# Modulation from the condition: plain fp32 products in four column tiles, the matrix in its own buffers

## The chip, the cores and the metric

One core of a Trainium2 chip runs the whole program. The metric is the device time of one execution in microseconds; lower is better. Three runs were made of the kernel before.

## The reference

Two transformer blocks on one sequence of 512 tokens of width 1024, all in fp32. The first block has two attentions (rotary differential and chunk-banded), a gated merge, cross attention to 256 memory tokens, a SwiGLU layer of width 2816 and a norm. The second block is modulated by a condition:

```python
mod = jax.nn.silu(c) @ w_ada[l] + b_ada[l]          # c: 1 x 1024, w_ada: 1024 x 6144
mod_c = jax.nn.silu(c_ctx) @ w_ada[l] + b_ada[l]    # the same matrix for the context
sh1, sc1, g1, sh2, sc2, g2 = jnp.split(mod[:, None, :], 6, axis=-1)
...
h_lat = _rms_norm(x, norm_mix[l]) * (1.0 + sc1) + sh1
```

It has a long convolution whose filter is made by a small sine network, a bidirectional gated linear attention, a projection, and a squared-ReLU layer of width 4096. What the change touches is `mod` and `mod_c`: two vectors of 1024 times one matrix of 1024 x 6144 (25.2 MB), whose result is needed first when the second block's first norm is applied.

## The kernel before, in words

Every large matrix goes through one path. It is cut into slabs of 128 columns with up to eight 128-row tiles (512 KB); a `Unit` is one slab. `U_` holds all units in the order in which every engine takes them. A slab goes through a ring of three slots:

- SP loads it into `raw` (`load`, line 509), once GpSimd is done with the slot's earlier slab (`low_done`).
- ScalarE rounds it to fp32r, `WH` (`high`, line 571), once TensorE is done with the slot (`unit_done`).
- GpSimd makes the rest, `WL = raw - WH` (line 552).
- TensorE adds up three products per row tile in fp32r: WH with the activation's high part, WH with its low part, WL with its high part (`unit`, line 1062): 24 products of 512 columns for a full slab. `half` (line 1074) and `piece` (line 1088) are the same in pieces.

The stages run one after the other. The stage `gu` (gate and up matrices of the SwiGLU layer) has 44 slabs, `dn0`, `dn1` and `dn2` (the down matrix) have eight each. After each `gu` unit VectorE takes the result from PSUM, scales it (lines 1942, 1944), ScalarE applies the silu (line 797), VectorE multiplies (line 1947), ScalarE and VectorE split the product into `fH` and `fL` (lines 800, 1648).

The modulation is done in the same ring. `w_ada` is the stage `ada` of 48 slabs, each two 128-row tiles of 512 columns. In `order` (lines 354 to 361) one `ada` unit stands behind each of the 44 `gu` units and behind the first four of `dn0`. The condition's silu, `cS` (128 x 8 x 2: vector and context), is split by VectorE into `cR`, high and low part, four columns (lines 1723 to 1725). TensorE's `ada(i)` (line 1366) multiplies each row tile of the slab's WH and WL by these four stationary columns, with 512 moving columns, into PSUM bank 5: four products a unit, and four units make one block of 512 columns. ScalarE's `keep_rows` copies the 4 x 512 result (line 788), sends it to DRAM (line 790), and reads all back at `dn0`'s fifth unit, turned so that 48 partitions have 128 columns each (line 825). After `dn1` TensorE transposes it (line 1411), and VectorE adds the bias and the low part's row (lines 1998, 2000).

At the border from the first block's cross attention to `gu`, TensorE waits for sums, then does the first `gu` unit in pieces (line 1088) and the statistics' sum (line 1035); ScalarE and VectorE finish the statistics, and ScalarE makes no weight copy until it has the square root (line 602). In `dn0` the filter network runs between the units: ScalarE issues the loads of its weights on its own DMA queue when `dn0`'s first unit is over (lines 806 to 812), and TensorE does its first product after the second unit (`filter_mm`, line 1374), the next ones after the fourth and sixth (line 1377), each behind a sine of ScalarE (line 821).

Other lines that the prediction names: 1187 (scores of the first attention, plain fp32: two products, one on partitions 0 to 63 and one on 64 to 127, into two banks), 1291 and 1310 (cross attention, plain fp32), 1525 (scores of the linear attention), 1543 (its states: plain fp32, 64 x 64 stationary, output on partitions 0 to 63 and 64 to 127 of bank 2 in turn, 128 columns), 1537 (128 x 128, before and behind 1543), 1420 (column sums, plain fp32, one moving column).

Of the kernel before, what the change touches and what calls it, by code (L numbers as in the profile page):

```python
# [22 lines left out]
ALU = mybir.AluOpType  # L23
# [42 lines left out]
SLOTS = 3  # L66
SLAB_KT = 8
# [49 lines left out]
def build(nc, t, out):  # L117
    ctx = ExitStack()
    with ctx:
# [32 lines left out]
        cR = place("cR", [P, DT, 4], F32R)  # L152
# [32 lines left out]
        rows = [z(f"rows{i}", kb, [4, S]) for i, kb in enumerate((93, 89))]  # L185
        mod_rows = hz("mod_rows", 0, [48, 4, P])
# [106 lines left out]
        mod_dram = nc.dram_tensor("mod_rows_dram", (4, 6 * D), F32, kind="Internal")  # L293
# [9 lines left out]
        def pairs(even, odd):  # L303
# [25 lines left out]
            Stage("ada", 48, DT, lambda i: w_ada[:, 2 * (i % 4):2 * (i % 4) + 2, i // 4 * S:(i // 4 + 1) * S]),  # L329
# [24 lines left out]
        for s_ in stages:  # L354
            if s_.name in ("gu", "dn0"):

                first = 0 if s_.name == "gu" else st["gu"].n
                for i in range(s_.n):
                    order.append((s_, i))
                    if first + i < st["ada"].n:  # L360
                        order.append((st["ada"], first + i))
            elif s_.name == "hyp":

                order += [(st[name], i) for name, i in WEAVE]
            elif s_.name == "ogp":
                order += [(s_, 0), (s_, 1), (st["grp"], 0), (s_, 2), (s_, 3)]
            elif s_.name not in ("ada", "uu", "grp"):
                order += [(s_, i) for i in range(s_.n)]
# [3 lines left out]
        for un in U_:  # L372
            if un.stage.name != "ada":
                un.out, un.bank = outs, un.stage.ring[made[un.stage.name] % len(un.stage.ring)]
                made[un.stage.name] += 1
                un.free = in_bank.get(un.bank, 0)
                outs += 1
                in_bank[un.bank] = outs
# [4 lines left out]
        def first_out(name):  # L383
# [22 lines left out]
        cond_ok, mod_in, mod_mm, lam_exp, lam_ok = (  # L406
            sem(n) for n in ("cond_ok", "mod_in", "mod_mm", "lam_exp", "lam_ok"))
        row_out = [sem(f"row_out{i}") for i in range(2)]
        scored, maxed, exped, normed, turned, kept, pv_done, pv_out = (
            {k: sem(f"{n}_{k}") for k in ("ab", "c")} for n in  # L410
            ("scored", "maxed", "exped", "normed", "turned", "kept", "pv_done", "pv_out"))
# [28 lines left out]
        def wide(a):  # L440

            return a[:].rearrange("p (a b) c -> p a (b c)", a=2)

# [14 lines left out]
        with_half = [g for g in range(STEPS) if g not in HEAD_STEPS]  # L458

# [25 lines left out]
        def _(sp):  # L485
# [15 lines left out]

            def load(lo, hi):
                for un in U_[lo:hi]:
# [4 lines left out]
                    dst = wide(raw[un.slot]) if s_.name == "ada" else raw[un.slot][:, 0:s_.kt, 0:width(s_)]  # L508
                    sp.dma_start(dst, s_.source(un.i)).then_inc(slab_in[un.slot], 16)
# [48 lines left out]
        def _(act):  # L558
# [221 lines left out]
            def keep_rows(i):  # L780

                if i % 4 == 3:
                    b = i // 4
                    if b >= 2:

                        act.wait_ge(row_out[b % 2], 16 * (b // 2))
                    act.wait_ge(unit_done, at["ada", i].u + 1)
                    act.activation(rows[b % 2][:], bank(5, S, 4), ACT.Copy).then_inc(row_kept, 1)
                    act.wait_ge(row_kept, b + 1)
                    act.dma_start(mod_dram[:, b * S:(b + 1) * S], rows[b % 2][:]).then_inc(row_out[b % 2], 16)  # L790

            for i in range(2 * FT):
# [8 lines left out]
                high(at["ada", i].u + SLOTS)  # L801
                keep_rows(i)
            for i in range(8):
# [11 lines left out]
                if i < 4:  # L815
                    high(at["ada", 2 * FT + i].u + SLOTS)
                    keep_rows(2 * FT + i)
# [201 lines left out]
        def _(pe):  # L1019
# [283 lines left out]
            def weigh_c(h):  # L1303
                pe.wait_ge(kept["c"], ST * (h + 1))
                if h:
                    pe.wait_ge(pv_out["c"], 2 * h)
# [11 lines left out]
            for s_ in range(C_ITEMS + 4):  # L1318
# [5 lines left out]
                if s_ == 10:  # L1324
                    begin(co0)
                    pe.wait_ge(pv_out["c"], 2)
# [4 lines left out]
                if s_ in (14, 16):  # L1331
                    pe.wait_ge(pv_out["c"], 4)
# [6 lines left out]
                if s_ == 18:  # L1339
                    for un in (co0, co1):  # L1340
                        pe.wait_ge(pv_out["c"], 6)
                        piece(un, oH, oL, (4, 5), 4, DT)

            pe.wait_ge(pv_out["c"], 2 * X_HEADS)
# [11 lines left out]
            def ada(i):  # L1356

                un = at["ada", i]
                pe.wait_ge(low_done, un.u + 1)
                if i % 4 == 0 and i:  # L1360

                    pe.wait_ge(row_kept, i // 4)
# [26 lines left out]
            pe.wait_ge(cond_ok, 1)  # L1389
            for i in range(2 * FT):  # L1390
# [5 lines left out]
                ada(i)  # L1396
            pe.wait_ge(res["gu"], 15)
            for i in range(8):
                unit(at["dn0", i], fH[:, 0:8], fL[:, 0:8])
                if i < 4:  # L1400
                    ada(2 * FT + i)
# [7 lines left out]
            pe.wait_ge(mod_in, 16)  # L1409
            for c in range(4):  # L1410
# [983 lines left out]
```

## Time and profile before

| | |
|---|---|
| median of 3 runs | 1798.88 us (1798.59 to 1800.63) |
| the profiled execution | 1800.05 us, span 1798.2 us |
| TensorE busy, products | 1729.0 us (96%) x7986 |
| VectorE | 895.9 us (50%) |
| ScalarE | 663.2 us (37%) |
| GpSimd | 770.9 us (43%) |
| mean granted TensorE clock | 0.984 |
| DMA | 179.86 MB, mean 100 GB/s |

The profile is one execution. Products on TensorE are pipelined: each is listed with its whole duration (0.39 us for one of 512 columns), and the next starts 0.23 us after it, so durations of neighbours overlap, and the distance from start to start is what one costs. The chain of waits follows the program back from its end: each piece is the instruction group that the next one waited for, or stood behind on its engine.

### The profile page before, as it was taken

What the parts mean: (1) busy time and instruction counts of PE and PEld (TensorE: products, weight loads), DVE (VectorE), ACT (ScalarE), POOL (GpSimd) and SP (SyncE); (2) the same over time, 40 slices, a digit from 0 to 9 for tenths busy, and PEclk for the clock granted to TensorE, in tenths of its full rate; (3) what the DMA queues carried; (4) which work ended last, traced back from release to release, by engine and by line L of the source; (5) the groups of instructions that cost most, each with busy time, mean ns of one, the idle gap of its engine ahead of it and who ended that gap; (6) DMA issues with size and microseconds to landing.
All of it is one profiled execution on the core that took longest, in us unless ns stands there. A gap on an engine that the chain in (4) does not pass through costs nothing.

```text
span 1798.2 us, 20290 instructions
## 1 busy us (share of the span) xinstructions
PE 1729.0 (96%) x7986; PEld 1354.5 (75%) x7986; DVE 895.9 (50%) x1233; ACT 663.2 (37%) x1036; POOL 770.9 (43%) x338
## 2 busy tenths in 40 slices
PE   5999999999999889999999998999999899999997
PEld 4777666677986667777777787787777688888886
DVE  5626656477424543333324655364565677162624
ACT  6124434355433434444442343463232323222222
POOL 2333222245741347777775333322133344444441
PEclk9999999999999989999999999999999899999999
DMA  5232211033541235555554222412034223333331
GB/s 186 74 90 71 59 47 51 27 123 106 156 137 47 59 94 164 165 164 168 163 170 136 82 72 78 145 53 59 24 88 126 85 83 102 97 94 95 104 95 59
DMA packets 293555, 179.86 MB, mean 100 GB/s; under 512 B 7961, under 2 KB 277811, under 8 KB 293204
## 3 DMA queue, kind: packets, MB, share of 16 engines
q1 hardware_dynamic: 291132, 170.63, 32.5%
q10 hardware_dynamic: 1768, 5.81, 1.0%
q0 software_dynamic: 560, 2.12, 0.3%
q8 instruction: 64, 1.05, 0.2%
q14 instruction: 31, 0.25, 0.0%
HBM read 174.22 MB, written 4.32 MB: 99 GB/s over the span
## 4 chain that ended last, share of the span: by engine, by line
PE 93%; DVE 3%; ACT 2%; issue 1%; DMA 1%; ACTq 0%; POOL 0%; DVEq 0%; SPq 0%
PE ps L1062 60%; PE ps L1074 13%; PE ps L1088 6%; PE ps L1366 2%; PE ps L1228 2%; PE ps L1196 1%; PE ps L1310 1%; PE ps L1208 1%; PE ps L1291 1%; PE ps L1187 1%; PE ps L1543 1%; PE ps L1141 0%; PE ps L1509 0%; DMA tok<-in_x_dram 0%; PE ps L1385 0%
## 5 line engine op out<-in xcount | busy, mean ns | idle before, releaser
L552 POOL TENSOR_TENSOR WL<-raw,WH 128x1024 fp32r<-128x1024 f32 (+2 forms) x330 | 768.5, 2337 | 987.8 <-ACT WH L571 987.6
L571 ACT ACTIVATE WH<-raw 128x1024 fp32r<-128x1024 f32 (+2 forms) x330 | 331.4, 1007 | 812.6 <-PE ps L1062 665.0
L1062 PE MATMUL ps<-hH,WH 128*128 128x512 f32 x808 | 205.9, 397 | 0.2 <-DVE qG L2051 0.2
L1062 PE MATMUL ps<-hL,WH 128*128 128x512 f32 x808 | 199.7, 389 | 0.0
L1062 PE MATMUL ps<-hH,WL 128*128 128x512 f32 x808 | 199.6, 389 | 0.0
L1062 PEld LDWEIGHTS ps<-hH,WH 128*128 128x128 f32 x808 | 150.8, 188 | 42.1 <-issue 3.8
L1062 PEld LDWEIGHTS ps<-hL,WH 128*128 128x128 f32 x808 | 151.0, 187 | 32.4
L1062 PEld LDWEIGHTS ps<-hH,WL 128*128 128x128 f32 x808 | 151.0, 187 | 32.2
L1074 PE MATMUL ps<-hH,WH 128*128 128x512 f32 x328 | 138.0, 421 | 0.7 <-DVE vfTc L2053 0.7
L1074 PE MATMUL ps<-hL,WH 128*128 128x512 f32 x328 | 129.1, 394 | 0.0
L1074 PE MATMUL ps<-hH,WL 128*128 128x512 f32 x328 | 129.0, 393 | 0.0
L1861 DVE SCALAR_TENSOR_TENSOR x<-ps,mod,x 128x512 f32<-128x512 f32 x40 | 30.0, 750 | 125.6 <-PE ps L1062 116.8
L1074 PEld LDWEIGHTS ps<-hH,WH 128*128 128x128 f32 x328 | 61.8, 188 | 32.4 <-issue 19.5
L1648 DVE TENSOR_TENSOR mL<-tmp,mH 128x512 fp32r<-128x512 f32 x32 | 78.0, 2438 | 7.6 <-ACT mH L1005 7.5
L1870 DVE TENSOR_TENSOR acc<-acc,tmp 128x512 f32<-128x512 f32 x40 | 67.5, 1689 | 28.6 <-ACT tmp L611 28.6
L1944 DVE TENSOR_TENSOR tmp<-ps,r 128x512 f32<-128x512 f32 x22 | 15.2, 691 | 118.8 <-PE ps L1062 118.8
L1074 PEld LDWEIGHTS ps<-hH,WL 128*128 128x128 f32 x328 | 62.0, 189 | 14.1
L1074 PEld LDWEIGHTS ps<-hL,WH 128*128 128x128 f32 x328 | 62.1, 189 | 10.9
L1062 PE MATMUL ps<-mH,WH 128*128 128x512 f32 x224 | 56.0, 392 | 0.0
L1062 PE MATMUL ps<-mH,WL 128*128 128x512 f32 x224 | 55.3, 389 | 0.0
L1062 PE MATMUL ps<-mL,WH 128*128 128x512 f32 x224 | 55.3, 389 | 0.0
L1648 DVE TENSOR_TENSOR fL<-tmp,fH 128x512 fp32r<-128x512 f32 x22 | 46.0, 2089 | 16.1 <-ACT fH L800 16.1
(461 smaller groups left out, 2767.8 us busy)
## 6 DMA issues: line engine op xcount, KB each, us to landing
raw<-in_w_in_dram SPq DMA_DIRECT2D x64, 512.0 KB, 3.6
raw<-in_w_mlp_dram SPq DMA_DIRECT2D x64, 512.0 KB, 3.9
raw<-in_w_ada_dram SPq DMA_DIRECT2D x48, 512.0 KB, 3.6
raw<-in_w_gate_up_dram SPq DMA_DIRECT2D x44, 512.0 KB, 3.6
raw<-in_w_out_dram SPq DMA_DIRECT2D x16, 512.0 KB, 3.7
raw<-in_w_ckv_dram SPq DMA_DIRECT2D x16, 512.0 KB, 3.9
raw<-in_w_down_dram SPq DMA_DIRECT2D x16, 448.0 KB, 3.5
raw<-in_k_dft_dram SPq DMA_DIRECT2D x17, 256.0 KB, 2.7
```

Of the source, the lines that this page charges most:

```text
L552: pool.tensor_tensor(WL[un.slot][:, 0:s_.kt, 0:n], raw[un.slot][:, 0:s_.kt, 0:n], WH[un.slot][:, 0:s_.kt, 0:n].bitcast(F32), ALU.subtract) ...
L571: act.activation(WH[un.slot][:, 0:s_.kt, 0:n], raw[un.slot][:, 0:s_.kt, 0:n], ACT.Copy).then_inc(high_done, 1)
L1062: ins = pe.matmul(dst, w[un.slot][:, q, 0:m], a[:, q, :], start=(k == 0), stop=(k == 3 * kt - 1))
L1074: ins = pe.matmul(bank(un.bank), w[un.slot][:, q, :], a[:, q, :], start=(q == 0 and e == 0), stop=(q == DT - 1 and e == 2))
L1088: ins = pe.matmul(bank(un.bank), w[un.slot][:, q, :], a[:, q, :], start=(c == 0 and e == 0), stop=(c == kt - 1 and e == 2))
L1187: ins = pe.matmul(ps[:, 3 + 2 * (n % 2) + c, 0:nk], qA[rows, h, q], kA[rows, h, 0:nk], start=True, stop=True)
L1196: ins = pe.matmul(bank(3 + n % 3, nk), qB[rows, h // 2, q], kB[rows, h // 2, 0:nk], start=True, stop=True)
L1228: ins = pe.matmul(ps[rows, 2, b * P:S], v[:, b, c], src[:, b, b * P:S], start=(b == 0), stop=True, skip_group_check=True)
L1366: ins = pe.matmul(bank(5, S, 4), cR[:, k, :], wide(w[un.slot])[:, q, :], start=(k == 0 and w is WH), stop=(k == DT - 1 and w is WL))
L1648: return dve.tensor_tensor(dl, src, dh.bitcast(F32), ALU.subtract)
L1861: dve.scalar_tensor_tensor(xm, bank(un.bank), scale(un.i), xm, ALU.mult, ALU.add).then_inc(bank_free, 1)
L1870: ins = dve.tensor_tensor(acc[:], acc[:], tmp[un.i % 2][:], ALU.add)
```

## The change

The stage `ada` leaves the slab ring, and its products become plain fp32 with the stationary operand `cS` itself (two columns; `cR` and its two VectorE instructions go). The matrix is loaded in twelve blocks of 512 columns, 2 MB each, into two buffers of 16 KB per partition (`ada_w`), which lie where `fH` and `fL` are written only late in the stage. SP issues each block as four transfers of 512 KB, two behind the load of a `gu` slab and two behind the next, for the slabs 3 to 26; from the third block on it first waits until TensorE is done with the block two before, and it waits until the block before has landed.

TensorE does a block at once after every second `gu` unit, from the fourth (i = 3) to the twenty-sixth (i = 25): 16 products of 256 columns. Four consecutive ones write to partitions 0, 32, 64 and 96 of bank 5: the even and odd row tile (q), each with the left and right half of the block (e). So each of the four places adds up four row tiles. `keep_rows` copies 128 x 256 and sends all of it to DRAM. The read back takes four transfers of the rows wanted, 24 partitions each, and the transposes become plain products with the identity that also add the even and odd part: eight where there were four. VectorE adds the bias in two instructions instead of four.

```diff
+ADA_PARTS = 12
-        cR = place("cR", [P, DT, 4], F32R)
-        rows = [z(f"rows{i}", kb, [4, S]) for i, kb in enumerate((93, 89))]
-        mod_rows = hz("mod_rows", 0, [48, 4, P])
+        rows = [z(f"rows{i}", kb, [P, 256]) for i, kb in enumerate((93, 89))]
+        mod_rows = hz("mod_rows", 0, [24, 8, P])
+        ada_w = [z(f"ada_w{i}", kb, [P, DT, S]) for i, kb in enumerate((28, 72))]
...
-            if s_.name in ("gu", "dn0"):
-
-                first = 0 if s_.name == "gu" else st["gu"].n
-                for i in range(s_.n):
-                    order.append((s_, i))
-                    if first + i < st["ada"].n:
-                        order.append((st["ada"], first + i))
...
+        def ada_after(i):
+            return i % 2 == 1 and 0 <= (i - 3) // 2 < ADA_PARTS
...
+            def load_ada(b, part):
+
+                if part == 0:
+                    if b < 2:
+                        sp.wait_ge(unit_done, first_u("gu"))
+                    else:
+                        sp.wait_ge(ada_done, b - 1)
+                    if b:
+
+                        sp.wait_ge(ada_in, 64 * b)
+                for k in (4 * part, 4 * part + 2):
+                    sp.dma_start(ada_w[b % 2][:, k:k + 2, :], w_ada[:, k:k + 2, b * S:(b + 1) * S]).then_inc(ada_in, 16)
...
+                    if s_.name == "gu" and 0 <= un.i - SLOTS < 2 * ADA_PARTS:
+                        load_ada((un.i - SLOTS) // 2, (un.i - SLOTS) % 2)
...
+            def keep_rows(b):
+
+                if b >= 2:
+
+                    act.wait_ge(row_out[b % 2], 16 * (b // 2))
+                act.wait_ge(ada_done, b + 1)
+                act.activation(rows[b % 2][:], bank(5, 256), ACT.Copy).then_inc(row_kept, 1)
+                act.wait_ge(row_kept, b + 1)
+                act.dma_start(mod_dram[:, b * 256:(b + 1) * 256], rows[b % 2][:]).then_inc(row_out[b % 2], 16)
...
-                high(at["ada", i].u + SLOTS)
-                keep_rows(i)
+                if ada_after(i - 1):
+                    keep_rows((i - 4) // 2)
...
-                    act.dma_start(mod_rows[:], mod_dram[:, :].rearrange("c (m p) -> m c p", p=P)).then_inc(mod_in, 16)
+                    for q in range(2):
+                        for e in range(2):
+                            first = 32 * (2 * q + e)
+                            act.dma_start(mod_rows[:, 4 * e + 2 * q:4 * e + 2 * q + 2, :],
+                                          mod_dram[first:first + 2, :].rearrange("c (m p) -> m c p", p=P)).then_inc(mod_in, 16)
...
-                for q in range(2):
-                    for w in (WH, WL):
-                        k = 2 * (i % 4) + q
-                        ins = pe.matmul(bank(5, S, 4), cR[:, k, :], wide(w[un.slot])[:, q, :],
-                                        start=(k == 0 and w is WH), stop=(k == DT - 1 and w is WL))
-                ins.then_inc(unit_done, 1)
+            def ada(b):
+
+                pe.wait_ge(ada_in, 64 * (b + 1))
+                if b:
+
+                    pe.wait_ge(row_kept, b)
+                for k in range(0, DT, 2):
+                    for q in range(2):
+                        for e in range(2):
+                            j = 32 * (2 * q + e)
+                            ins = pe.matmul(ps[j:j + 2, 5, 0:256], cS[:, k + q, :], ada_w[b % 2][:, k + q, e * 256:(e + 1) * 256],
+                                            start=(k == 0), stop=(k == DT - 2), skip_group_check=True)
+                ins.then_inc(ada_done, 1)
...
-                ada(i)
+                if ada_after(i):
+                    ada((i - 3) // 2)
...
-            for c in range(4):
-                ins = pe.transpose(ps[:, 5, c * 48:(c + 1) * 48], mod_rows[:, c, :], ident[0:48, 0:48])
+            for c in range(2):
+                for e in range(2):
+                    for q in range(2):
+                        ins = pe.matmul(ps[:, 5, c * 48 + e * 24:c * 48 + e * 24 + 24], mod_rows[:, 4 * e + 2 * q + c, :], ident[0:24, 0:24],
+                                        start=(q == 0), stop=(q == 1), skip_group_check=True)
```

## Rows read from the trace of the kernel before

**Rows 1.** The page, busy time of each engine (share of the span).

```profile
PE 1729.0 (96%) x7986; PEld 1354.5 (75%) x7986; DVE 895.9 (50%) x1233; ACT 663.2 (37%) x1036; POOL 770.9 (43%) x338
```

**Rows 2.** Who waited for whom, 640 to 1060 us: total, times, longest (us).

```profile
ACT WH L571 <- PE ps L1062: 219.9, 61, 8.6
...
PE ps L1366 <- POOL WL L552: 2.0, 1, 2.0
```

**Rows 3.** Chain of waits, 600 to 1100 us: start, us, what.

```profile
659.31 1.69 PE ps L1366 x4
661.00 6.47 PE ps L1062 x24
...
668.40 5.45 PE ps L1062 x24
673.85 0.93 PE ps L1366 x4
...
940.16 4.36 DMA fout<-in_filt_wout_dram
...
945.64 7.27 PE ps L1062 x24
```

**Rows 4.** By stretch: length, PE, PEld, DVE, ACT, POOL busy, clock, DMA share, GB/s.

```profile
670.00:930.00 260.00, 260.00 (x1142) 197.28 (x1142) 84.73 (x82) 109.62 (x132) 204.42 (x82) 1.00 0.55 165
960.00:964.00 4.00, 4.00 (x15) 2.55 (x15) 2.71 (x4) 1.87 (x3) 3.47 (x2) 1.00 0.97 312
```

**Rows 5.** Groups of instructions, 640 to 1060 us: busy us, mean ns, idle before.

```profile
L552 POOL TENSOR_TENSOR WL<-raw,WH 128x1024 fp32r<-128x1024 f32 (+1 forms) x114 | 279.2, 2467 | 145.7 <-ACT WH L571 145.7
L571 ACT ACTIVATE WH<-raw 128x1024 fp32r<-128x1024 f32 (+1 forms) x113 | 117.2, 1040 | 227.4 <-PE ps L1062 219.9 <-issue 4.3 <-DMA raw<-in_w_gate_up_dram 2.6
...
L1366 PE MATMUL ps<-WL,cR 128*4 128x512 f32 x96 | 38.5, 401 | 0.0
...
L788 ACT ACTIVATE rows<-ps 4x512 f32<-4x512 f32 x12 | 6.9, 572 | 0.0
```

**Rows 6.** Chain of waits, 520 to 556 us: plain fp32 passes on the whole array.

```profile
525.28 0.86 PE ps L1291 x4
...
551.92 3.44 PE ps L1310 x8
```

**Rows 7.** TensorE in order of time: start, us, line, shapes, passes.

```profile
203.99 1.13 PE L1187 MATMUL ps<-kA,qA 64*128 64x512 f32 x4
205.05 0.50 PE L1074 MATMUL ps<-hH,WH 128*128 128x512 f32 x1
205.39 0.40 PE L1074 MATMUL ps<-hL,WH 128*128 128x512 f32 x1
...
1271.43 0.38 PE L1537 MATMUL ps<-vG,att 128*128 128x128 f32 x2
1271.74 0.66 PE L1543 MATMUL ps<-state,qin 64*64 64x128 f32 x8
1272.33 0.38 PE L1537 MATMUL ps<-vG,att 128*128 128x128 f32 x1
```

**Rows 8.** In order of time: the first filter product and the first sine.

```profile
944.57 1.07 PE L1374 MATMUL ps<-zT,fw 33*64 33x512 f32 x2 [1.84 <-DMA fout<-in_filt_wout_dram]
...
954.93 0.61 ACT L821 ACTIVATE fh<-ft 64x512 f32<-64x512 f32 x1
```

**Rows 9.** Chain of waits: the transposes of the rows, and eight one-column passes.

```profile
1031.08 0.37 PE ps L1411 x4
...
1041.22 0.79 PE ps L1420 x8
```

**Rows 10.** TensorE in order of time, and one stretch, in the linear attention.

```profile
1258.81 2.05 PE L1525 MATMUL ps<-qin,kin 64*128 64x128 f32 x16
...
1265.02 2.05 PE L1525 MATMUL ps<-qin,kin 64*128 64x128 f32 x16 [1.22 <-DVE att L2184]
...
1267.00:1270.50 3.50, 3.50 (x10) 2.73 (x10) 1.98 (x3) 0.00 (x0) 0.00 (x0) 0.52 0.00 0
```

More of the change, by code:

```diff
@@ L366, in build @@
                 order += [(s_, 0), (s_, 1), (st["grp"], 0), (s_, 2), (s_, 3)]
-            elif s_.name not in ("ada", "uu", "grp"):
+            elif s_.name not in ("uu", "grp"):
                 order += [(s_, i) for i in range(s_.n)]
@@ L372, in build @@
         for un in U_:
[L373 to L378, printed above, removed]
+            un.out, un.bank = outs, un.stage.ring[made[un.stage.name] % len(un.stage.ring)]
+            made[un.stage.name] += 1
+            un.free = in_bank.get(un.bank, 0)
+            outs += 1
+            in_bank[un.bank] = outs
         def first_u(name):
@@ L405, in build @@
             sem(n) for n in ("rot_done", "roped", "v_turned", "v_kept", "sig_done"))
-        cond_ok, mod_in, mod_mm, lam_exp, lam_ok = (
-            sem(n) for n in ("cond_ok", "mod_in", "mod_mm", "lam_exp", "lam_ok"))
+        ada_done, mod_in, mod_mm, lam_exp, lam_ok = (
+            sem(n) for n in ("ada_done", "mod_in", "mod_mm", "lam_exp", "lam_ok"))
+        ada_in = sem("ada_in")
         row_out = [sem(f"row_out{i}") for i in range(2)]
-        scored, maxed, exped, normed, turned, kept, pv_done, pv_out = (
+        scored, maxed, exped, normed, turned, kept, pv_done = (
             {k: sem(f"{n}_{k}") for k in ("ab", "c")} for n in
-            ("scored", "maxed", "exped", "normed", "turned", "kept", "pv_done", "pv_out"))
+            ("scored", "maxed", "exped", "normed", "turned", "kept", "pv_done"))
+        pv_out = sem("pv_out")
         out_a, out_b = sem("out_a"), sem("out_b")
@@ L507, in load @@
                     s_ = un.stage
-                    dst = wide(raw[un.slot]) if s_.name == "ada" else raw[un.slot][:, 0:s_.kt, 0:width(s_)]
-                    sp.dma_start(dst, s_.source(un.i)).then_inc(slab_in[un.slot], 16)
+                    sp.dma_start(raw[un.slot][:, 0:s_.kt, 0:width(s_)], s_.source(un.i)).then_inc(slab_in[un.slot], 16)
+                    if s_.name == "gu" and 0 <= un.i - SLOTS < 2 * ADA_PARTS:
+                        load_ada((un.i - SLOTS) // 2, (un.i - SLOTS) % 2)
             load(0, first_u("gate"))
@@ L778, in _ @@
             stat("ffn", r)
[L780 to L790, printed above, removed]
+            def keep_rows(b):
[5 more added lines that the diff above has]
+                act.dma_start(mod_dram[:, b * 256:(b + 1) * 256], rows[b % 2][:]).then_inc(row_out[b % 2], 16)
             for i in range(2 * FT):
@@ L1720, in values @@
                 dve.wait_ge(v_turned, c0 + st[name].n)
-            dve.wait_ge(silu_c, 2)
-            own.step(dve.tensor_scalar(cR[:, :, 0:2], cS[:], 1.0, None, ALU.mult))
-            dve.tensor_tensor(cR[:, :, 2:4], cS[:], cR[:, :, 0:2].bitcast(F32), ALU.subtract).then_inc(cond_ok, 1)
             values("va", 0)
@@ L1915, in out_c @@
                     c = 2 * h + j
-                    rest(bank(b_), oH[:, c, :], oL[:, c, :]).then_inc(pv_out["c"], 1)
-                dve.wait_ge(pv_out["c"], 2 * h + 2)
+                    rest(bank(b_), oH[:, c, :], oL[:, c, :]).then_inc(pv_out, 1)
+                dve.wait_ge(pv_out, 2 * h + 2)
             each("cq", query_tile, 0, 3)
@@ L1997, in _ @@
             for c in range(2):
-                own.step(dve.tensor_tensor(mod[:, :, c], ps[:, 5, c * 48:(c + 1) * 48],
-                                           vec[:, VEC_AT["b_ada_2"]:VEC_AT["b_ada_2"] + 48], ALU.add))
-                ins = dve.tensor_tensor(mod[:, :, c], ps[:, 5, (2 + c) * 48:(3 + c) * 48], mod[:, :, c], ALU.add)
-                if c == 0:
-                    own.step(ins)
+                ins = dve.tensor_tensor(mod[:, :, c].rearrange("p (b e m) -> p e b m", e=2, m=2),
+                                        ps[:, 5, c * 48:(c + 1) * 48].rearrange("p (e b m) -> p e b m", e=2, m=2),
+                                        vec[:, VEC_AT["b_ada_2"]:VEC_AT["b_ada_2"] + 48].rearrange("p (b e m) -> p e b m", e=2, m=2),
+                                        ALU.add)
             ins.then_inc(mod_ok, 1)
```

31 lines of the change are left out of this document (9 added, 22 removed).

## The prediction

> **What bounds the kernel now.** I read the page's busy table first: TensorE is busy 96% of the span, no other computing engine over 50% [rows 1]. Busy alone decides nothing, so next came who waits for whom in the stretch that the change touches, 640 to 1060 us: the longest wait is one for TensorE (ScalarE's weight copies waited 219.9 us for products to free their slot), and TensorE's modulation products waited 2.0 us in all, for GpSimd [rows 2]. Then the chain of waits: from 661 to 935 us it is nothing but TensorE, a unit of 24 products at 5.45 us and four modulation products at 0.93 us in turn, without an issue gap [rows 3]. So in the gate/up stage TensorE's own time is the stage's time, and each microsecond taken out of it there leaves the path. GpSimd works 204 us of the 260 there and the DMA engines 0.55 of the time, at 165 GB/s [rows 4].
>
> **Removed on TensorE.** 192 modulation products of 512 columns with four stationary columns (96 on the high halves, as the 96 on the low ones in [rows 5]). On the chain they are 48 groups of four at 0.93 us [rows 3]: 44.6 us. One of them stands behind the pause of 2.0 us: it starts at 659.3, when GpSimd has its low half, and takes 1.69 in place of 0.93, the unit after it 6.47 in place of 5.45 [rows 2, 3]; they ran at half clock for a while. In the new order the three slots filled before the statistics are three gate/up units, 16 us of work for TensorE from about 651 us, and the fourth one's low half is there at 659.3, where the group's is now. Pause and slow stretch go: 2.0 + 0.8 + 1.0 = 3.8 us.
>
> **Added on TensorE.** Twelve bursts, one after every second unit from the fourth on. A burst is 16 plain fp32 products of 256 columns, and a plain fp32 product is two passes: 4 passes of 256 columns stand as 0.86 us, 8 of 512 as 3.44 us [rows 6], so 0.215 us a pass of 256 and half that for 128. 32 passes one behind the other are 6.88 us. The four products of a group write partitions 0, 32, 64 and 96, so they lie in four column tiles. The trace has no four tiles, but it has two. Line 1543 alternates between two column halves, with the same rows: eight passes of 128 columns (0.11 us each alone) take 0.59 us from start to next start, not 0.86; line 1187, with two row halves, takes 1.06 us for four passes of 512 columns where one behind the other they were 1.72 [rows 7]. Without the edges (below) that is half of the serial time: both tiles ran at once. In line 1187 that holds though the program issues each product's two passes one after the other. I take four tiles at once, as that is the same mechanism and the nearest row is column tiling in one bank: 8 slots of 0.215, 1.72 us. Bounds: no overlap, 6.88; two tiles only, 3.44.
> The Trainium skill ("TensorE: Matmul & The Clock Gate", Part 3, What overlaps) gives 2.38 times for three column tiles and 3.07 times for four row tiles, not 4; by the latter a burst's passes would be an estimated 2.24 us, and the sum 6 us worse.
> The edges: going from 128 columns to a narrower tile costs 0.09 us (1271.43, two passes, to 1271.74), the first load and the drain 0.15 (0.59 less four slots of 0.11), the first product back on the whole array 0.11 (205.05 to 205.39 against 0.23) [rows 7]: 0.35. A burst is 2.07 us, twelve are 24.8 us. The burst wants a pass every 0.054 us; line 1543's eight in 0.44 us came as fast.
>
> **The down stage.** Two groups stood before the first filter product. That product waits for its weights, whose transfer is issued by ScalarE behind nine small ones after the stage's first unit; it is issued at about 940.2, lands 4.36 us later, and TensorE had stood 1.84 us [rows 3, 8]. Without the two groups TensorE only comes 1.86 us earlier and stands 3.7: gain 0 (the landing may come up to 1.5 us sooner with less traffic: low end only). After the pause the unit takes 7.27 instead of 5.45 at half clock, today as well; I keep that. Two more groups are behind it: 1.86 of the 44.6 counts, 1.86 does not. Next the second filter product: its sine is done at 955.5 [rows 8] and it is wanted 5.45 us after the unit that ends at 952.9 [rows 3], so nothing is late.
>
> **Turning the rows.** Four transposes (0.37 us) become eight plain products, 16 passes; eight passes of one column took 0.79 us [rows 9], so 1.6, and 0.1 more of edges: +1.3 us, on the path in the down stage.
>
> **Costed at nothing.** GpSimd loses 48 low halves, ScalarE 48 copies: neither is on the path, gate/up units come every 5.45 us or more and need 2.5 and 1.0 [rows 5]. The row copy (0.57 us now, [rows 5]) follows the silu, some 2.2 us after the unit behind a burst; the next burst wants the bank 5.45 us after it: 3 us of cover; without it each burst would pay the difference. VectorE loses two conversions early on and two of four small sums late; ScalarE's queue gets four row reads where it had one, in a stage where it has one copy a unit to make. The new 1 KB rows for all partitions write 1.5 MB more.
> **Loads.** SP issues the same 48 modulation transfers of 512 KB, but in half the stage: four with every two slabs, behind the slab. SP then waits until the burst two before is done, and the next slab stands behind that wait and 1 MB. The slab is issued up to 4 us late and then stands behind that 1 MB: 1.5 MB are 5 us at the 300 GB/s that 165 at a share of 0.55 come to when full, so it lands within 8; ScalarE wants it 10.9 us after, TensorE two units later still. Twelve blocks and 24 slabs are 37.7 MB in 24 x 5.45 + 24.8 = 156 us: 243 GB/s, a share of 0.81 by the ratio of [rows 4]. The engines have carried 312 GB/s at 0.97 [rows 4]. Cover is there, but it is half gone.
>
> **Sum.** -44.6 - 3.8 + 24.8 + 1.9 (the two groups given back) + 1.3 = -20.4 us. Against the profiled execution's 1800.05 that is 1779.6; its time lies 1.2 above the median of the runs, 1798.88, so 1778.5.
>
> **Rivals.**
> *Only two tiles at a time* (each product's second pass holds up the ones behind it, or the four streams from the same partitions are too many). For: the trace has never more than two. Against: there both were fully at work [rows 7]. Then 3.44 + 0.35 = 3.79 a burst, 45.5 in all: 1799.2, the same. The Trainium skill says on that page that products start and end in strict order of the program; by that rule each second pass blocks the next product and this rival is the forecast. Line 1187's four passes in two slots disagree: by strict order they were three slots. 10%.
> *No overlap (the other side).* Products with the same 128 rows share one stream of weights and columns, and every burst costs 6.88 + 0.35 = 7.2 us: 86.8 in all, 1840.5. It decides from 3.77 us a burst on, the break-even (2.07 + 20.4 / 12). Against it: line 1543 has the same rows for both tiles. 5%.
> *The clock falls.* A burst fills 8 of 128 columns. Sixteen narrow passes (2.05 us) behind a pause of 1.22 us were followed by 3.5 us at 0.52 of the clock; the same sixteen without a pause kept the full clock [rows 10]. One such fall costs 1.75 us. If every second burst causes one, 10.5 us: 1789; if all, 1799.5. A burst has no pause beside it, which speaks against. 10%.
> *The loads become the bound.* If this mix of transfers gets only three quarters of the 300 GB/s, 225, the 37.7 MB take 168 us, 12 more: 1790.5. The 312 GB/s speak against. 4%.
>
> **Chances.** Forecast 71% (its own range 1771 to 1787: the landing 1.5 sooner, a burst cheaper by 0.2 or dearer by 0.5, one half-clock stretch of 1.75 more or two fewer at the pauses that stay); the rivals 10, 5, 10 and 4%. The range reaches 1771 to 1798, which takes in the loads and most of the clock. About 0.2%, 3.6 us, is what a measurement of this kernel tells from no change. Faster by over that: 0.71 + 0.04 + most of the clock = 0.85; same 0.09; slower 0.06.
>
> **What would show it.** The chain after: units of 5.45 us back to back and twelve bursts of about 2.07 (32 passes, starts in groups of four); 3.8 or 7.2 shows a rival. PEclk 1.0 through the stage, or not. DMA share near 0.8 over the first 24 units, 0.4 behind; gate/up slabs landing some 8 us after issue behind modulation loads, and no wait of TensorE for ScalarE's copies. The pause at 657 gone; the one before the first filter product longer by up to 1.9. I am wrong if TensorE shows waits inside the gate/up stage, or if a burst is much off 2 us.

## The result

The changed kernel takes 1779.9 us (median of five runs, the lowest 1778.71) against 1798.88 us for the one before; the ratio is 0.9888, with a 95% interval of 0.9875 to 0.9902. Forecast were 1778.5 us and a range of 1771 to 1798. One of the five, the one that was profiled, took 6667.16 us, with TensorE's products 0.84 us apart in place of 0.23 at a recorded clock of 1.00, for a reason that is not known. So all rows of the kernel after are from another execution of the same kernel (experiment 1 below): 1779.05 us, span 1777.2. The span before was 1798.2, so 21.0 us have to be accounted for.

The busy table and the slices of the page after; [rows 1] answer to them.

```profile
PE 1707.7 (96%) x8190; PEld 1346.0 (76%) x8190; DVE 891.9 (50%) x1229; ACT 614.4 (35%) x988; POOL 647.5 (36%) x290
...
PEclk9999999999999999999999999999999899999999
DMA  5232121134552157873333223421133233333331
```

TensorE is still busy 96% of a shorter span, so the kernel is bound as before; GpSimd and ScalarE lost their 48 conversions each; but for TensorE's old pause of 2.0 us for GpSimd, the time didn't come from there. The DMA row shows the loads crowded into the slices from 666 to 800 us and thinner behind. Next the chain of waits after, over the stretch that the change touches; [rows 3, 9] answer to it. It starts with the first gate/up unit, which is done in pieces (L1094).

```profile
642.44 6.45 PE ps L1094 x24
...
649.75 16.37 PE ps L1068 x72
666.11 1.84 PE ps L1372 x32
667.95 11.12 PE ps L1068 x48
...
808.67 1.84 PE ps L1372 x32
810.51 103.62 PE ps L1068 x456
...
918.99 4.25 DMA fout<-in_filt_wout_dram
923.28 1.07 PE ps L1380 x2
924.35 12.71 PE ps L1068 x48
937.06 1.00 PE ps L1383 x2
...
1007.91 1.89 PE ps L1418 x16
1009.80 9.74 PE ps L1068 x42
1019.55 0.79 PE ps L1428 x8
```

Behind it three units (72 products) run without a pause where the old one of 2.0 us was. Then comes a period that repeats: a burst of 32 passes (L1372), 1.84 us, and two units, 11.12 us, 12.96 in all. Two units cost 10.90 by [rows 3], so a burst costs 2.06 us. The twelfth starts at 808.67; from there TensorE has nothing but units. The two places of waiting that matter, TensorE's first filter product in order of time, then the whole waits over 640 to 1060 us ([rows 8] and [rows 2] answer to them):

```profile
923.28 1.07 PE L1380 MATMUL ps<-zT,fw 33*64 33x512 f32 x2 [3.73 <-DMA fout<-in_filt_wout_dram]
```

```profile
ACT WH L578 <- PE ps L1068: 269.3, 66, 11.0
POOL WL L559 <- ACT WH L578: 256.9, 69, 16.2
```

ScalarE waits for TensorE longer than before (269.3 us against 219.9) and GpSimd waits for ScalarE: both have more slack. The pause ahead of the filter product is 3.73 us, where it was 1.84. The stretches after, as in [rows 4]:

```profile
650.00:810.00 160.00, 160.00 (x979) 120.04 (x982) 56.31 (x53) 46.75 (x64) 60.99 (x26) 1.00 0.70 229
810.00:910.00 100.00, 100.00 (x451) 82.45 (x441) 37.66 (x37) 29.73 (x37) 43.90 (x19) 1.00 0.33 97
```

The clock is 1.00 through the bursts, TensorE is busy in every microsecond of it, and the DMA engines are at 0.70, not full.

### The profile page after: what moved, and what is told of

Its sections match the earlier page's. It is cut to its first block, busy times and chain, and to the rows that moved or that the text cites. A ratio compares the mean times of both kernels' runs of the same rounds, so it can differ in the third digit from the quotient of the medians.

```text
span 6665.3 us, 20564 instructions
## 1 busy us (share of the span) xinstructions
PE 6627.1 (99%) x8190; PEld 3652.8 (55%) x8190; DVE 848.3 (13%) x1229; ACT 622.2 (9%) x988; POOL 634.1 (10%) x290
## 4 chain that ended last, share of the span: by engine, by line
PE 99%; DVE 0%; ACT 0%; DMA 0%; issue 0%; ACTq 0%; SPq 0%; DVEq 0%
PE ps L1068 62%; PE ps L1080 16%; PE ps L1094 6%; PE ps L1234 2%; PE ps L1202 2%; PE ps L1214 1%; PE ps L1372 1%; PE ps L1193 1%; PE ps L1316 1%; PE ps L1297 1%; PE ps L1160 1%; PE ps L1147 1%; PE ps L1031 1%; PE ps L1168 0%; PE ps L1533 0%; PE ps L1391 0%
## 5 line engine op out<-in xcount | busy, mean ns | idle before, releaser
L1068 PE MATMUL ps<-hH,WH 128*128 128x512 f32 x808 | 770.8, 1205 | 0.0
L1068 PE MATMUL ps<-hH,WL 128*128 128x512 f32 x808 | 749.5, 1178 | 0.0
L1068 PE MATMUL ps<-hL,WH 128*128 128x512 f32 x808 | 749.2, 1176 | 0.0
L1068 PEld LDWEIGHTS ps<-hH,WH 128*128 128x128 f32 x808 | 392.8, 490 | 345.5 <-issue 340.3
L1068 PEld LDWEIGHTS ps<-hH,WL 128*128 128x128 f32 x808 | 398.8, 494 | 319.8 <-issue 319.8
L1068 PEld LDWEIGHTS ps<-hL,WH 128*128 128x128 f32 x808 | 398.0, 493 | 321.0 <-issue 321.0
L1080 PE MATMUL ps<-hH,WH 128*128 128x512 f32 x328 | 481.6, 1468 | 0.0
L1080 PE MATMUL ps<-hL,WH 128*128 128x512 f32 x328 | 456.5, 1392 | 0.0
L1080 PE MATMUL ps<-hH,WL 128*128 128x512 f32 x328 | 455.7, 1389 | 0.0
L1080 PEld LDWEIGHTS ps<-hH,WH 128*128 128x128 f32 x328 | 204.3, 623 | 231.9 <-issue 227.4
L1080 PEld LDWEIGHTS ps<-hL,WH 128*128 128x128 f32 x328 | 235.2, 717 | 103.7 <-issue 103.5
L1080 PEld LDWEIGHTS ps<-hH,WL 128*128 128x128 f32 x328 | 215.3, 656 | 127.9 <-issue 126.6
L1068 PE MATMUL ps<-mH,WH 128*128 128x512 f32 x224 | 193.4, 1104 | 0.0
L1068 PE MATMUL ps<-fL,WH 128*128 128x512 f32 x176 | 151.5, 1091 | 0.0
L1068 PE MATMUL ps<-fH,WH 128*128 128x512 f32 x176 | 151.4, 1092 | 0.0
L1068 PE MATMUL ps<-fH,WL 128*128 128x512 f32 x176 | 150.6, 1098 | 0.0
```

Of the source, the lines that this page charges most:

```text
L1068: ins = pe.matmul(dst, w[un.slot][:, q, 0:m], a[:, q, :], start=(k == 0), stop=(k == 3 * kt - 1))
L1080: ins = pe.matmul(bank(un.bank), w[un.slot][:, q, :], a[:, q, :], start=(q == 0 and e == 0), stop=(q == DT - 1 and e == 2))
```

## Where the 21.0 us went

By the two chains, from the start of one piece to that of the next (of the chain before, the pieces at 643.39, 960.22 and, [rows 9], 1041.22 us; after, at 642.44, 937.06 and 1019.55):

| from, to | before | after | difference | forecast |
|---|---|---|---|---|
| start to the first gate/up unit | 643.39 | 642.44 | -0.95 | 0 |
| from there to the second filter product | 316.83 | 294.62 | -22.21 | -21.7 |
| from there to the eight one-column passes behind the turned rows | 81.00 | 82.49 | +1.49 | +1.3 |
| the rest of the kernel | 756.98 | 757.65 | +0.67 | 0 |

The second row is all of the modulation, the pause at its start and the pause at the filter. The half microsecond by which it beats the forecast is at two stretches of half clock: in the first unit, 6.45 us where it was 6.71, and behind the filter's pause, 1.6 us lost where it was 1.8. The first and the last row, -0.95 and +0.67, hold next to nothing of the change (two conversions of VectorE early, two small sums late). They are of the size by which single executions differ: in the eleven traces here the piece of the first row starts between 642.44 and 645.11 us. Experiment 4 shows one place in the last row.

## The experiments

Each is timed beside runs of the kernel before on its own chip (medians 1799.5, 1799.3 and 1800.6 us in the three groups), so ratios are to be compared. Four questions: do all four tiles run at once, and on what does it depend (1 to 3, 9, 10); what does the filter's pause cost (4, 5); what do the small added pieces cost (6, 7); are the loads near their bound (8).

**1. The changed kernel again.**

> The changed kernel once more, for its trace beside the others of this call. My theory (four column tiles at once): twelve bursts of about 2.07 us from the last unit's end to the next unit's start, units of 5.45 us, no wait of TensorE in the gate/up stage, granted clock 1.00 there, a pause of about 3.7 us before the first filter product; time 1778 to 1781. Rival, two tiles at once: bursts of 3.8 us, and the time would have had to come from elsewhere, such as shorter pauses. Rival, cheaper bursts but a lower clock: bursts under 2 us with stretches at half clock in the stage.

Measured: 1779.82 us, ratio 0.989 [0.9875, 0.9905]. The rows of after above are its own.

**2. Two tiles' products in turn, then the other two's.**

```diff
-                for k in range(0, DT, 2):
-                    for q in range(2):
+                for q in range(2):
+                    for k in range(0, DT, 2):
                         for e in range(2):
```

> The same 16 products of a burst in another order: those of the first two column tiles first, in turn, then those of the other two. If a tile works on its own product beside the others, only two are busy at once: 16 slots of 0.215 us and 0.35 for the edges, 3.8 us a burst, 12 x 1.72 = 20.6 us more than the changed kernel, about 1800.5. If the order of the program decides nothing (TensorE looks far ahead), the time stays at 1780. If already the changed kernel has only two tiles at once, it stays at 1780 too, with bursts of 3.8 in both.

**3. One tile after the other.**

```diff
-                for k in range(0, DT, 2):
-                    for q in range(2):
-                        for e in range(2):
+                for q in range(2):
+                    for e in range(2):
+                        for k in range(0, DT, 2):
```

> The same 16 products, the four of one column tile one behind the other (eight passes in one tile in a row). My theory: the passes of one tile are serial, so 32 slots less what overlaps at the three borders between tiles: 6.2 to 6.9 us and 0.35, 12 x 4.5 to 5.2 = 54 to 62 us more than the changed kernel, 1834 to 1842. Rival (the gain is not from overlap but from the narrow tile or the plain fp32 itself): within a few us of the changed kernel.

Measured: 1789.96 us (0.9947 [0.9927, 0.9967]) and 1810.8 us (1.0063 [1.0043, 1.0083]). Both are slower than the changed kernel, so the order of the program matters and the tiles are what makes it fast; but both are some 10 and 25 us faster than was expected of them. A burst in the chains, first of experiment 2, then of 3:

```profile
680.18 2.70 PE ps L1372 x32
```

```profile
683.89 4.42 PE ps L1372 x32
```

In slots of 0.216 us a burst is 8.5 slots in the changed kernel, 12.5 here with two tiles in turn (16 expected) and 20.5 with one after the other (32 expected). The weight loads, one to a pass and started with it or up to a slot ahead of it, show how. Loads by stretch of 0.86 us, four slots, from the first of a burst on (length, loads' busy time and number, clock, DMA share, GB/s): the changed kernel first, then experiment 3.

```profile
678.99:679.85 0.86, 0.42 (x20) 1.00 0.40 132
679.85:680.71 0.86, 0.32 (x12) 1.00 0.17 50
```

```profile
683.81:684.67 0.86, 0.34 (x5) 1.00 0.04 13
684.67:685.53 0.86, 0.35 (x8) 1.00 0.00 0
685.53:686.39 0.86, 0.35 (x8) 1.00 0.00 0
686.39:687.25 0.86, 0.35 (x8) 1.00 0.00 0
687.25:688.11 0.86, 0.26 (x3) 1.00 0.00 0
```

The changed kernel starts four passes in every slot and has the next four loads made ahead: 20 loads, then the other 12. In experiment 3 four passes go alone (5 loads with the one made ahead), and then two in every slot, though the program has all eight passes of the first tile ahead of the second's. The passes start at 683.816, 684.031, 684.247 and 684.463 us, then at 684.679 and 684.685, 684.895 and 684.900, and so on. Two that start 6 ns apart can't be one tile's, so the second tile's first pass runs beside the first tile's fifth, ahead of its sixth. The reading that gives these numbers: each tile can have four passes issued and unfinished; a fifth waits in the program's order and holds up everything behind it. With one tile after the other the second starts when the first one's eighth pass is let in, at slot 4, the third at 8, the fourth at 12, and its eight passes end at slot 20. With two in turn the other two start at slot 4 and end at 12. For the changed kernel's order a tile need hold only the two passes of one product, as line 1187 showed [rows 7]; the other orders ask for more. Experiments 9 and 10 try this reading where it was not made.

**9. Two products of a tile in a row, and 10. three, then one.**

```diff
-                for k in range(0, DT, 2):
+                for ks in ((0, 2), (4, 6)):
                     for q in range(2):
                         for e in range(2):
...
+                            for k in ks:
```

In experiment 10 the first line has ((0, 2, 4), (6,)).

> The changed kernel with the 16 products of a burst ordered so that each of the four tiles gets two products (four passes) in a row before the next tile's turn, twice round. Theory (the four tiles run side by side, each with up to four passes issued and not ended, and only a fifth holds up what stands behind it; it gives 20 slots for the burst in the order of one tile after another, and 12 for two tiles at once, where 20.5 and 12.5 were seen): no pass is held up, the burst stays at 8 slots and 2.08 us, the time at the changed kernel's 1779.8, within 1.5. Rival (a pass for another tile starts only when all passes ahead of it in the program's order have started): three of every four passes of a tile wait for their own tile, the second tile starts with slot 4 and so on, some 26 slots of 0.216 us, 5.9 us a burst and 12 x 3.8 = 45 us more: 1825.

> The same with three products (six passes) of a tile in a row, and one in the second round. Theory (four passes a tile, the fifth holds up the rest): the sixth pass of a tile is let in at slot 2, so the tiles start at slots 0, 2, 4 and 6 and the last of them ends at slot 14: 14 x 0.216 + 0.24 = 3.26 us a burst, 1.18 more than 2.08, 12 x 1.18 = 14.2 us: 1794.0, within 2.5. Rival A (a tile holds eight passes or more, and the one-tile-at-a-time order was slow for another reason, such as a whole accumulation having to close): no difference, 1779.8. Rival B (strict order of starts): over 26 slots, 1825 and more.

Measured: 1780.77 us (0.9888 [0.9869, 0.9907]) and 1795.75 us (0.9974 [0.9964, 0.9984]). A burst in the chains, 9 and then 10:

```profile
681.31 1.86 PE ps L1373 x32
```

```profile
682.29 3.13 PE ps L1373 x32
```

8.6 slots and 14.5 slots, where 8 and 14 and the half slot that every order has were expected; strict order, over 26, is out, and so is a tile that holds eight passes. All five orders follow from one rule: 8, 8, 12, 14 and 20 slots, plus half of one. Worked out in the same way, a tile that holds three passes gives 8, 11, 13, 17 and 23 slots, and one that holds five 8, 8, 11, 11 and 17, so only four fits. It fits within the burst too: in experiment 10 the passes that start in each slot are 1, 1, 2, 2, 3, 3, 3, 3, 4, 4, 2, 2, 1, 1 by the rule, and the trace has the same. The times follow too: (3.13 - 1.84) x 12 = 15.5 us over the changed kernel's 1779.8 is 1795.3. Whether it is four passes or two products that a tile holds these orders can't tell, since every product here is two passes.

**4. The filter's products one unit later, in the changed kernel.** Its weights then have landed when TensorE comes to them.

```diff
-                if i in (1, 3, 5):
-                    filter_mm(i // 2)
-            filter_out(0)
+                if i in (2, 4, 6):
+                    filter_mm(i // 2 - 1)
...
+                if i == 0:
+                    filter_out(0)
```

The sines on ScalarE and the layer on VectorE move by one unit with it.

> The changed kernel with the three filter layers one unit later each (after the third, fifth and seventh unit of the first down stage in place of the second, fourth and sixth), and the filter's first output products after the first unit of the next stage. My theory: the two groups of modulation products that stood before the first filter product were given back as a longer pause (3.7 us for 1.84) and half a clock after it (1.8 us), so both go: 5 us less than the changed kernel, about 1774.5. Rival: the filter's chain is as late one unit later, because the pause only moves to a later layer's sine or to the first output products: within 1.5 us of the changed kernel.

**5. The same edit in the kernel before.**

> The kernel before, with the filter's three products, and its output product, one to two units later (as in the run before this one that moved them in the changed kernel), and the modulation left as it was. Theory (the changed kernel's first filter product, with three quarters of the removed pause's cover gone, gave back 1.9 us, and TensorE ran slower for a stretch behind that pause): here the pause to remove is only the 1.84 us one, with its slow stretch of 1.8 us, so about 3.6 us come off: 1795 to 1796.5, ratio 0.997 to 0.9985; and the step from this kernel to the changed one with the same edit is 22 to 23 us rather than 19 to 20. Rival (the edit's gain has nothing to do with what the change did at the filter: it is the same for both kernels): about 7 us come off here as well, 1792, ratio 0.996.

Measured: experiment 4 1772.66 us, 0.9848 [0.9831, 0.9864]; experiment 5 1795.75 us, 0.9979 [0.9969, 0.9988]. The chains of experiment 4, its first burst and from the twelfth on, and of experiment 5, its first modulation group behind the pause, the filter, and the turning of the rows:

```profile
669.34 1.84 PE ps L1372 x32
...
811.90 1.84 PE ps L1372 x32
813.74 114.48 PE ps L1068 x504
928.22 1.00 PE ps L1380 x2
929.22 11.12 PE ps L1068 x48
...
1005.75 1.89 PE ps L1419 x16
```

```profile
658.20 1.87 PE ps L1366 x4
...
947.03 0.93 PE ps L1366 x4
947.96 1.00 PE ps L1374 x2
948.95 5.69 PE ps L1062 x24
...
1026.43 0.37 PE ps L1412 x4
```

Pause and slow stretch are gone in both. From the first burst (666.11 after, 669.34 here) to the turning of the rows it is 341.80 us in the changed kernel and 336.41 here: 5.39 less, the 3.73 of the pause and the 1.6 by which 12.71 was over 11.12. In the kernel before the like distance (659.31 to 1031.08, [rows 3, 9]) is 371.77 us and in experiment 5 368.23: 3.54 less. The difference between the two, 1.85, is what the change gave back at that pause; the 1.9 of the forecast's sum is shown.

The median of experiment 4 fell by 7.2 us, not 5.4, and the traces don't settle where the other 1.8 us are. One place shows how much a stretch that no edit touched can move. At some 1050 us every kernel here has a pause of 0.81 us, where TensorE waits for VectorE, and behind it come 24 products. The chain there, changed kernel, experiment 4, the kernel before, and experiment 9:

```profile
1054.88 8.47 PE ps L1068 x24
```

```profile
1052.37 5.57 PE ps L1068 x24
```

```profile
1076.30 7.10 PE ps L1062 x24
```

```profile
1056.95 7.14 PE ps L1068 x24
```

The mean granted clock over these pieces is 0.65, 1.00, 0.78 and 0.78: the same products fell to half clock for long, not at all, or for a while. Each row is one execution. Experiment 9 has behind the bursts the changed kernel's program, and so has experiment 8 (7.16 us), so the 8.47 looks like that execution's and not the kernel's, which with one trace of each isn't shown. Nor can the 2.9 us between the first two rows explain the medians: experiment 4's trace is of its longest execution, 1775.2 us, and its span is only 3.8 us below the changed kernel's. Against that one it gains 5.4 us up to the turning of the rows and 3.2 from there to the end of these 24 products, and loses 3.2 ahead of the first burst and 1.6 behind the 24, places where nothing was changed. What the edit is worth is therefore read from its own stretch. In the same way 1.4 us of the table's last row (8.47 against 7.10) are the clock of these two executions; without them the row would be below zero.

**6. The rows turned by two products.** The eight products of 24 rows are replaced by two of 96 rows with a selection matrix that VectorE makes by one addition (on top of experiment 4).

```diff
-                for e in range(2):
-                    for q in range(2):
-                        ins = pe.matmul(ps[:, 5, c * 48 + e * 24:c * 48 + e * 24 + 24], mod_rows[:, 4 * e + 2 * q + c, :], ident[0:24, 0:24],
-                                        start=(q == 0), stop=(q == 1), skip_group_check=True)
+                ins = pe.matmul(ps[:, 5, c * 48:(c + 1) * 48], mod_rows[:, c, :], sel[0:96].rearrange("p e m -> p (e m)"),
+                                start=True, stop=True, skip_group_check=True)
```

> The changed kernel with the filter's products later, and the stored rows turned and summed by 2 products of 96 rows with a selection matrix (4 passes) in the place of 8 products of 24 rows (16 passes). Theory (each pass of the turning costs its own time, 1.89 us for 16 in a trace of the changed kernel): the stretch falls to 0.4 to 0.8 us and the time by 1.0 to 1.4 us against the kernel that has only the filter's edit, ratio to the kernel before about 0.984. Rival (the turning waits for something else, the rows' landing or the conversion of the next piece, and the passes are free): no difference, and a pause of TensorE of about 1 us stands at that place.

Measured: 1773.0 us, 0.9852 [0.9835, 0.9868]. The chain at that place:

```profile
1003.92 0.38 PE ps L1420 x4
1004.30 9.62 PE ps L1070 x42
```

0.38 us against 1.89, and 9.62 against 9.74: 1.63 us are gone, without a pause in their place. In the medians nothing is gone (1773.0 against 1772.66), and why is open: 1.6 us are 0.09%, the two ratios have intervals of 0.3%, and experiment 4's runs alone spread over 4.2 us. In the two traces the stretch above takes 1.6 us more here (7.17 against 5.57), but it is one execution of each, and as a whole this one is 2.1 us shorter. The rival (that the passes are free) is refuted by the chain, not by the time.

**7. Bursts in pairs.** On top of experiment 6, two bursts after every fourth unit, two banks in turn.

```diff
-            return i % 2 == 1 and 0 <= (i - 3) // 2 < ADA_PARTS
+            return i % 4 == 1 and 5 <= i <= 25
...
-                            ins = pe.matmul(ps[j:j + 2, 5, 0:256], cS[:, k + q, :], ada_w[b % 2][:, k + q, e * 256:(e + 1) * 256],
+                            ins = pe.matmul(ps[j:j + 2, (5, 4)[b % 2], 0:256], cS[:, k + q, :], ada_w[b % 2][:, k + q, e * 256:(e + 1) * 256],
...
-                    ada((i - 3) // 2)
+                    ada((i - 5) // 2)
+                    ada((i - 5) // 2 + 1)
```

> The same with the twelve bursts made as six pairs (every fourth unit, two banks in turn). Theory (a burst costs eight slots of 0.215 us and an edge of 0.35 us for the switch between the two kinds of products): six of twelve edges go, 6 x 0.35 = 2.1 us less than the run before it, a pair takes 3.8 us; ratio about 0.983. Rival A (the edge belongs to each burst's own start, its four first weight loads): a pair takes 4.1 to 4.2 us and the time doesn't change. Rival B (8 KB a partition of modulation matrix wanted within one short stretch: the loads are late for the second of the pair): TensorE pauses ahead of bursts, and the time rises by 2 us or more.

Measured: 1771.58 us, 0.9841 [0.9826, 0.9856], the fastest kernel here. The chain, and the one wait of TensorE for a chunk (in order of time):

```profile
703.45 3.57 PE ps L1375 x64
707.01 22.02 PE ps L1071 x96
```

```profile
679.53 1.91 PE L1375 MATMUL ps<-ada_w,cS 128*2 128x256 f32 x32 [0.55 <-DMA ada_w<-in_w_ada_dram]
```

A pair and four units take 25.59 us, where two single periods are 25.92: 0.33 us for each edge that goes, 0.35 forecast. Six of them are 2.0 us; the second chunk of the first pair was 0.55 us late, and the rest, 1.4 us, is what the medians show (1.8 in the spans). The interval doesn't separate it from experiment 6; the chain does. The clock stayed at 1.00 through the first pair too, with its pause of 0.55 us.

**8. More loads.** Behind each of the last nine chunks another 640 KB come in that nobody reads.

```diff
+        dump = [z(f"dump{h}", kb, [P, n]) for h, (kb, n) in enumerate(((90, 384), (91.5, 384), (94, 256), (95, 256)))]
...
+                for h in range(2 if b > 2 else 0):
+                    sp.dma_start(dump[2 * part + h][:], w_ada[:, 4 * part + h, b * S:b * S + dump[2 * part + h].shape[-1]]).then_inc(ada_in, 16)
```

> The changed kernel with 640 KB of further loads behind each of the last nine modulation chunks (into space that nobody reads, on the same queue), so that some 300 GB/s rather than 250 come in over this stretch. Theory (the loads are covered: a slab lands some 7 us after its issue and isn't wanted for 10.9): slabs land later, up to 9 us, and the time stays within 1 us of the changed kernel's, ratio 0.989. Rival (the loads are all but the bound, as peaks of 0.99 in the engines' share suggest): each of nine bursts is 1 us or more late, and the time rises by 9 us or more, ratio 0.994 and up.

Measured: 1779.47 us, 0.9885 [0.987, 0.99], the changed kernel's time. The DMA view of 700 to 800 us: mean rate, and the median time from issue to landing of a slab; the changed kernel, then experiment 8.

```profile
DMA packets 26018, 25.25 MB, mean 253 GB/s; under 512 B 872, under 2 KB 18353, under 8 KB 26012
...
raw<-in_w_gate_up_dram SPq DMA_DIRECT2D x16, 512.0 KB, 6.3
```

```profile
DMA packets 31348, 30.78 MB, mean 308 GB/s; under 512 B 1376, under 2 KB 23662, under 8 KB 31342
...
raw<-in_w_gate_up_dram SPq DMA_DIRECT2D x16, 512.0 KB, 7.2
```

22% more bytes, slabs 0.9 us later, no pause. The cover of the loads held, with room beyond what the change uses.

## Why the prediction was right, step by step

- **Removed on TensorE** (-44.6 and -3.8). Right. In the chain after no line of the old products is left and 72 products stand where the pause was; the -22.21 us of the table's second row against -21.7 leaves no room for another term above half a microsecond, apart from terms that cancel. Piece by piece it is -44.6 for the groups, -3.8 for the old pause, +24.7 for the bursts, +1.9 for the pause at the filter and -0.5 of clock, -22.3 in all.
- **Added on TensorE** (2.07 us a burst). 2.06. The forecast put it together as 1.72 for eight slots and 0.35 of edges; measured are 1.84 from the first pass to the next product and 0.22 in the units behind. Experiment 7 measures the edge by itself, 0.33. The step "four tiles at once, as that is the same mechanism" was the one that decided, and was taken from rows with two tiles [rows 7]; experiments 1 to 3, 9 and 10 show it, and show too that it hangs on the order: one tile after the other would have been slower than the kernel before, 1.0063 [1.0043, 1.0083].
- **The rival of two tiles** rested on a rule of the Trainium skill ("TensorE: Matmul & The Clock Gate", Part 3, What overlaps), by which products start and end in the order of the program. The traces disagree: 32 passes in 8.5 slots, and in experiment 3 passes of the second tile beside the first one's fifth to eighth. By the same page's 3.07 times for four row tiles (Part 3, Measured speedup vs the span model) the passes would take an estimated 2.24 us. They took less: 6.88 us in series became 1.84 to the start of the next product, 3.7 times, or 2.06 with all of the edge, 3.3 times. My own numbers for experiments 2 and 3 took the rule's side as far as a second pass of one's own tile goes, and missed by 10 and 25 us: I had not thought of a tile that holds passes of several products.
- **The down stage** (+1.9). Right in size, 3.73 us of pause against 3.7 forecast, and shown by experiments 4 and 5 (1.85). The slow unit behind it stayed, 1.6 us against 1.8.
- **Turning the rows** (+1.3). 1.89 us against 0.37 and +1.49 over the stretch. The passes cost 0.1 to 0.2 more than forecast.
- **Costed at nothing.** Held. The row copy ends at 688.54 us and the next burst wants the bank at 692.03: 3.5 us of cover, 3 forecast (the copy takes 0.37 us, not 0.57, with half the columns). GpSimd and ScalarE have more slack.
- **Loads.** Covered, but by other numbers than forecast: 229 GB/s at a share of 0.70 over 650 to 810 us, where 243 at 0.81 were worked out. By that ratio the full engines move 327 GB/s, not 300. Slabs land 7.1 us after issue over the bursts, 8 forecast. SP stood 65 us waiting for chunks to land before it issued the next, which the forecast had not listed; nothing came of it, since no pause of TensorE stands in the chain. Its own view, 640 to 930 us:

```profile
SPq L504 <- DMA ada_w<-in_w_ada_dram: 65.1, 11, 7.3
```

- **The clock.** It stayed at 1.00 through all twelve bursts, as argued from their having no pause beside them; no run put a burst behind a pause longer than the 0.55 us of experiment 7. Where the clock does decide a microsecond or two is behind the pauses that the kernel has anyway, and there it went either way from one execution to the next.

The sum came to -20.4 us, where the medians differ by 19.0 and the two profiled spans by 21.0: by either it is within 1.5 us.

## What to carry to other kernels

Products with few stationary columns can share TensorE four at a time, in column tiles of one bank, even when all use the same 128 rows; issue them in turn over the tiles, at most two fp32 products of a tile in a row, since a fifth pass for one tile stops the program for all. Gather the bursts: each costs a third of a microsecond at its edges. Here every burst stood between other work of TensorE; what one would do behind a longer pause no run shows. And when work is taken out ahead of a transfer that TensorE waits for, move the waiting product as well: here that was worth 5.4 us, more than a quarter of the change.

## What was not expected

- Each of the four tiles behaves as if it took four passes (or two products) before it holds up the others: bursts of 8.5, 8.6, 12.5, 14.5 and 20.5 slots for five orders of the same 32 passes.
- The DMA engines carried up to 393 GB/s in single slices of 3.4 us at a share of 0.9 or more (the view tells no more, and so not the 0.99 that experiment 8's expectation names); [rows 4] had 312 at 0.97. The modulation's loads come in pieces of 2 KB, the slabs' in pieces of 512 bytes. The DMA view of 663 to 800 us:

```profile
DMA  7289849936991899199739954992799099819991
GB/s 260 41 306 330 273 104 378 388 103 160 380 380 36 252 372 332 16 331 391 224 42 367 393 159 118 379 380 84 200 377 370 15 283 380 296 22 335 392 309 57
```

- The same 24 products behind the same 0.81 us pause took 5.57 to 8.47 us in the traces, at a mean clock of 1.00 to 0.65, and by experiments 8 and 9 that looks like the execution's doing more than the kernel's. Medians of four runs don't resolve an edit of some 1.5 us beside that, so its size has to be read from the chain at its own place.
